# A two-block transformer kernel on one core: another order of feature tiles, steps moved between stages, and a rotation kept on one engine

## What is computed

```python
def first_block(x, c, ctx, c_ctx, ...):          # DEPTH = 2 layers
    for i in range(DEPTH):
        ml = modulation(c, w_mod[i], b_mod[i]);  mc = modulation(c_ctx, ...)
        hl = modulate(rmsnorm(xl, g_pre_mix[i]), ml[0], ml[1])
        hc = modulate(rmsnorm(xc, g_pre_mix[i]), mc[0], mc[1])
        # in-projection, conv branches, attention over context + latent keys, output product w_o
        xl_new = xl + ml[2] * rmsnorm(y_l, g_post_mix[i])
        h2 = modulate(rmsnorm(xl_new, g_pre_mlp[i]), ml[3], ml[4])
        xl_new = xl_new + ml[5] * rmsnorm(sqrelu_mlp(h2, w_mlp_in[i], w_mlp_out[i]), g_post_mlp[i])
        # the same for the context stream, except in the last layer
def second_block(x, ...):                        # 2 hybrid layers: delta rule, pooling, sparse attention
        q = apply_rope(rms_norm(qc, q_norm), cos_a, sin_a)
        k = apply_rope(rms_norm(kc, k_norm), cos_a, sin_a)
        return x + merged @ w_out
```

## Time and profile before

| what | value |
|---|---|
| three executions | 2986.65, 2987.75, 2988.89 us |
| median | 2987.75 us |
| profiled execution, its own time | 2985.46 us |
| its span in the trace | 2984.2 us |
| mean granted clock of TensorE | 0.984 of full |
| TensorE (PE) busy | 2854.2 us, 96% |
| DVE, ACT, POOL busy | 1361.4, 1125.9, 1309.4 us |
| read from memory | 286.93 MB, 97 GB/s over the span |

### The profile page before, as it was taken

One profiled execution on the slowest core, in us unless ns is written; L12 is line 12 of the kernel. 1 busy time (PEld: TensorE's weight loads), 2 busy tenths in 40 slices (PEclk: granted clock), 3 DMA queues, 4 the chain that ended last, 5 costly groups with the idle time before them and its releaser, 6 DMA issues.

```text
span 2984.2 us, 40937 instructions
## 1 busy us (share of the span) xinstructions
PE 2854.2 (96%) x16292; PEld 2354.3 (79%) x16292; DVE 1361.4 (46%) x2490; ACT 1125.9 (38%) x1909; POOL 1309.4 (44%) x860
## 2 busy tenths in 40 slices
PE   7789999999999999989999899999999999999999
PEld 6576777988888785778888787888878778888777
DVE  5447654232111475633111356775543368666432
ACT  4343554553322443543322344332333344323332
POOL 4253236774444441244444343344634443437433
PEclk9999999999999999999999999999999999999999
DMA  6833214553233323122333222111222221212222
GB/s 236 303 132 121 86 43 131 176 158 107 92 99 99 121 67 124 58 71 86 98 99 95 67 97 75 57 57 50 85 76 84 85 85 53 70 52 71 78 72 91
DMA packets 81982, 291.68 MB, mean 98 GB/s; under 512 B 9216, under 2 KB 9600, under 8 KB 81408
## 3 DMA queue, kind: packets, MB, share of 16 engines
q1 hardware_dynamic: 81792, 289.06, 29.3%
HBM read 286.93 MB, written 2.10 MB: 97 GB/s over the span
## 4 chain that ended last, share of the span: by engine, by line
PE 81%; DVE 11%; issue 3%; POOL 2%; ACT 2%; DMA 0%; SPq 0%; POOLq 0%; DVEq 0%; ACTq 0%
PE ps L595 61%; PE ps L568 6%; DVE ps L2186 4%; PE ps L738 3%; PE ps L623 2%; PE ps L759 2%; PE ps L990 1%; POOL t L2814 1%; PE ps L927 1%; PE ps L1001 1%; PE ps L863 1%; DVE t L2010 1%; POOL t L2834 1%; PE ps L1168 1%; DVE t L2476 1%
## 5 line engine op out<-in xcount | busy, mean ns | idle before, releaser
L595 PE MATMUL ps<-t,t 128*128 128x512 f32 (+3 forms) x9936 | 2215.4, 381 | 30.5 <-DVE t L1969 12.6
L595 PEld LDWEIGHTS ps<-t,t 128*128 128x128 f32 x9936 | 1783.3, 189 | 377.6 <-issue 42.9
L2814 POOL TENSOR_TENSOR t<-t,t 128x1024 fp32r<-128x1024 f32 (+3 forms) x444 | 1046.0, 2360 | 1101.6 <-ACT t L1303 1048.3
L1303 ACT ACTIVATE t<-t 128x1024 fp32r<-128x1024 f32 (+3 forms) x444 | 457.6, 1034 | 877.4 <-PE ps L595 826.1
L568 PE MATMUL ps<-t,t 128*128 128x128 f32 (+2 forms) x1676 | 245.8, 284 | 53.6 <-DVE t L2010 20.6
L568 PEld LDWEIGHTS ps<-t,t 128*128 128x128 f32 (+2 forms) x1676 | 196.9, 144 | 103.7 <-DVE t L2010 21.6
L2289 DVE TENSOR_TENSOR ps<-ps,t 128x512 f32<-128x512 f32 (+1 forms) x96 | 57.2, 605 | 335.3 <-ACT t L1591 331.5
L2302 DVE TENSOR_TENSOR t<-ps,t 128x512 f32<-128x512 f32 x60 | 40.9, 691 | 217.6 <-PE ps L595 217.5
L2834 POOL TENSOR_TENSOR t<-t,t 128x4 f32<-128x4 f32 (+2 forms) x93 | 85.7, 922 | 77.1 <-DVE t L1973 39.1
L2186 DVE SCALAR_TENSOR_TENSOR ps<-t,t,ps 128x512 f32<-128x512 f32 (+1 forms) x174 | 116.1, 667 | 6.7 <-ACT ps L1506 0.9
L738 PE MATMUL ps<-t,t 96*128 96x384 f32 (+1 forms) x320 | 108.9, 464 | 3.9 <-DVE t L2054 1.5
(11 more groups left out here) (258 smaller groups left out, 2471.6 us busy)
## 6 DMA issues: line engine op xcount, KB each, us to landing
t<-in_wbig SPq DMA_DIRECT2D x412, 512.0 KB, 3.5
t<-in_wmod SPq DMA_DIRECT2D x96, 512.0 KB, 6.6
t<-in_wbig SPq DMA_DIRECT2D x16, 416.0 KB, 3.2
t<-in_wbig SPq DMA_DIRECT2D x14, 256.0 KB, 2.7
t<-in_wbig SPq DMA_DIRECT2D x8, 332.0 KB, 2.8
t<-in_wbig SPq DMA_DIRECT2D x6, 384.0 KB, 3.0
t<-in_x SPq DMA_DIRECT2D x1, 2048.0 KB, 8.1
out<-t SPq DMA_DIRECT2D x8, 256.0 KB, 2.1
```

What stands on the lines that cost most here:

```text
L595: m = p.matmul(out, lhs, rhs, start=kk == 0 and n == 0, stop=kk == tiles - 1 and n == 2)
L1303: a.activation(c.hi(w), c.raw(w), ACT.Copy).then_inc(w_hi.h, w_hi.up(("cut", w)))
L2814: g.tensor_tensor(c.lo(w), c.raw(w), c.hi(w).bitcast(F32), ALU.subtract).then_inc(w_lo.h, w_lo.up(("cut", w)))
```

## The change

Eight parts, made in the programs of all engines alike:

1. `prep(l0)` and `prep(mc0)` go through the tiles in the order 4 to 7, 0 to 3; `high` of each waits only for the unit of `wo` that read that tile last; the first product of the stage starts with tile 4. Three more steps of the prep are placed inside `project`. Beside `project(c0)` the side steps go at rate 0.65 instead of 0.5.
2. `residual` multiplies by the row once before it takes the mean and three times after, and waits for the root only right before each addition.
3. In the last group of an MLP, the first step of the next prep on ACT, DVE and POOL (squares, mean, root) is placed ahead of the second in-product; TensorE's step stays.
4. Modulation group (0,4) moves from `heads(c0)` to the end of `mix(c0)`; (1,5) from `heads(l0)` to behind `zt` of c1; (1,10) and (1,11) from `heads(l1)` to behind `project(l1)`. Three of them get other ring slots and waits.
5. The row product for ml1 moves from ahead of `prep(ml1)` into `mlp(ml1)`.
6. During `zt` of c1 the units are cut 2, 2, 1 and 0 ahead instead of 2, 2, 2 and 2.
7. All four multiplications of the kc and qc rotations are DVE's.

```diff
+def first_tile(stage):
+    return 4 if stage[0] == "wo" or stage in (("cf", "l0"), ("w1", "mc0", 0, 0)) else 0
+def prep_order(n):
+    return (4, 5, 6, 7, 0, 1, 2, 3) if n in ("l0", "mc0") else tuple(range(8))
+def only(steps, n):
+    for _ in range(n):
+        next(steps)
+        yield
...
     def mod_slots(self, i, g):
-        return [4 * (n if n < 4 else 4 if n > 12 and n % 2 else 2 if n in (5, 7, 9) else 0) + q for q in range(4)]
+        return [4 * (n if n < 4 else {17: 3, 23: 1}.get(n, 4) if n > 12 and n % 2 else 2 if n in (5, 7, 9) else 0) + q
+                for q in range(4)]
...
 # ACT, POOL: product_gemm
-            cut(u, (1, 1, 2, 2)[kh] if stage == ("cf", "c0") else AHEAD)
+            cut(u, {("cf", "c0"): (1, 1, 2, 2), ("zt", "c1"): (2, 2, 1, 0)}.get(stage, (AHEAD,) * 4)[kh])
...
 # ACT: prep
             A.wait_ge(dve, ("pn", n, k))
+            if read and prep_order(n)[0]:
+                A.wait_ge(gemm, ("w", c.of[read][prep_order(n).index(k) // 2]))
...
-        if read:
+        ks = prep_order(n)
+        if read and not ks[0]:
             A.wait_ge(gemm, ("end", read))
-        high(0)
+        high(ks[0])
...
 # ACT, DVE, POOL: mlp
             for h in range(2):
+                if g == 3 and h:
+                    next(ahead, None)
                 yield from product_gemm(("w1", n, g, h), ...)
-            yield from weave(down(g), ahead, rate) if g == 3 else down(g)
+            yield from weave(down(g), chain((0,), ahead), rate) if g == 3 else down(g)
...
 # DVE: residual
         if row is not None:
-            for t in range(nt - 1):
-                gained(n, 1, t)
+            gained(n, 1, 0)
         V.wait_ge(act, ("ysq", n, 1, nt - 1))
...
         if row is not None:
-            gained(n, 1, nt - 1)
+            for t in range(1, nt):
+                gained(n, 1, t)
             V.wait_ge(dve, ("yg", n, 1, nt - 1))
-        V.wait_ge(pool, ("rr", n))
         for t in range(nt):
             for _ in range(apart):
                 yield
+            V.wait_ge(pool, ("rr", n))
...
 # DVE: rotate
+        if crossed is None:
+            v.tensor_tensor(tmp[2], p2, co, ALU.mult).then_inc(dve.h, dve.up())
+            v.tensor_tensor(tmp[3], p1, si, ALU.mult).then_inc(dve.h, dve.up())
...
-        V.wait_ge(pool, crossed)
+        if crossed is not None:
+            V.wait_ge(pool, crossed)
...
 # every engine's main program (PE's shown)
-    steps = beside(mix("c0"), g, (1, 2, 3, 9, 11, 13, 15))
+    steps = beside(beside(mix("c0"), g, (1, 2, 3, 9, 11, 13, 15)), mods(0, 4, 5, [2, 6]), (48,))
...
-    rest = onward(weave(heads("c0"), mods(0, 4, 12, [6, 7]), 0.45, -1.0), 2 * NH + 2)
+    rest = onward(weave(heads("c0"), mods(0, 5, 12, [6, 7]), 0.45, -1.0), 2 * NH + 2)
...
-    run(weave(project("c0"), both(rest, g, 4), 0.5))
-    next(g)
+    run(beside(weave(project("c0"), both(rest, g, 4), 0.65), only(g, 3), (11, 14, 15)))
     run(beside(weave(mix("l0"), g, 0.5), mods(1, 0, 1, [2, 6]), (56,)))
-    rest = onward(beside(heads("l0"), mods(1, 1, 6, [6, 7]), (4, 5, 12, 13, 20)), 4 * NH + 2)
+    rest = onward(beside(heads("l0"), mods(1, 1, 5, [6, 7]), (4, 5, 12, 13)), 4 * NH + 2)
...
-    run(weave(project("l0"), both(rest, g, 4), 0.45))
-    next(g)
+    run(beside(weave(project("l0"), both(rest, g, 4), 0.45), only(g, 3), (21, 24, 26)))
...
     keys = onward(mix("c1"), 8)
+    run(mods(1, 5, 6, main[2:4]))
     g = onward(prep("l1"), 5)
...
-    rest = onward(beside(heads("l1"), mods(1, 6, 12, [6, 7]), (4, 5, 12, 13, 20, 21)), 4 * NH + 2)
+    rest = onward(beside(heads("l1"), mods(1, 6, 10, [6, 7]), (4, 5, 12, 13)), 4 * NH + 2)
...
     run(weave(project("l1"), rest, 0.4))
-    row_of("ml1", 1, 1, 0)
+    run(mods(1, 10, 12, main[2:4]))
     g = onward(prep("ml1"), 5)
...
 # SP: fetch_mod
-        if i == 1 and g % 2:
+        if i == 1 and g in (1, 3, 7, 9):
             S.wait_ge(gemm, ("end", ("sb", "l1" if g > 6 else "l0")))
+        if i == 1 and g == 5:
+            S.wait_ge(dve, ("x", "l0", 3))
+        if i == 1 and g == 11:
+            S.wait_ge(turned, ("put", "l1", 0, 3))
```

More of the change, by code:

```diff
@@ L42, in mix @@
         for key in (("zt",) if n == "c1" else ("cf", "zt", "sc", "sb")):
-            block((key, n), "w_in", (i,), 0, 8, IN1[key])
+            for row in (512, 0) if (key, n) == ("cf", "l0") else (0, 512):
+                block((key, n), "w_in", (i,), row, 4, IN1[key])
         if n != "c1":
@@ L569, in turns, with product_gemm @@
         last.then_inc(turned.h, turned.up(*events))
-    def product_gemm(stage, mode, parts, T, w, tiles, ready, freed, first=0, banks=(0, 1, 2, 3)):
+    def product_gemm(stage, mode, parts, T, w, tiles, ready, freed, banks=(0, 1, 2, 3)):
         aH, aL = parts
@@ L1889, in act_program @@
     g = prep("l0")
-    run(weave(project("c0"), both(rest, g, 4), 0.5))
-    next(g)
+    run(beside(weave(project("c0"), both(rest, g, 4), 0.65), only(g, 3), (11, 14, 15)))
     run(beside(weave(mix("l0"), g, 0.5), mods(1, 0, 1), (56,)))
-    rest = onward(beside(heads("l0"), mods(1, 1, 6), (4, 5, 12, 13, 20)), 4 * NH + 2)
+    rest = onward(beside(heads("l0"), mods(1, 1, 5), (4, 5, 12, 13)), 4 * NH + 2)
     row_of("l0")
@@ L3001, in mlp @@
             for h in range(2):
+                if gr == 3 and h:
+                    next(ahead, None)
                 yield from product_gemm(("w1", n, gr, h), 4, 8, lambda b: None)
-            yield from weave(down(gr), ahead, rate) if gr == 3 else down(gr)
+            yield from weave(down(gr), chain((0,), ahead), rate) if gr == 3 else down(gr)
     def bc(col):
@@ L3156, in pool_program @@
     onward(steps, 2)
-    first = beside(mix("c0"), steps, (1, 2, 3, 9, 11, 13, 15))
+    first = beside(beside(mix("c0"), steps, (1, 2, 3, 9, 11, 13, 15)), mods(0, 4, 5), (48,))
     for n in (2, 3):
```

98 lines of the change are left out of this document (46 added, 52 removed).

## The result

The changed kernel takes 2968.26 us in the median of 4 runs (2965.27 to 2975.67), the kernel before 2988.32 beside it (4 runs, 2986.65 to 2990.79). The ratio is 0.9932, 95% interval 0.9921 to 0.9944: 20 us less. The profiled execution took 2965.27 us with a span of 2963.9, against 2985.46 and 2984.2 before.

What follows compares the result with a forecast made beforehand. TensorE, busy 2854.2 of 2984.2 us, was taken as the bound: its work plus some 130 us of waits. The terms summed to -27.5, from 2985.5 to 2958, on the median's scale 2960; range 2951 to 2973.

Steps and rivals of the forecast that it cites:

- root wait and squares ahead (D): In mc0: later root wait gains 2.3 us of TensorE's 2.66 wait; squares before ACT's cut cost net 2.4.
- heads(l0) without (1,5) (C): In heads(l0): the modulation group taken out gives back 1.93 us and 0.3 of transpose.
- heads(l1), ml1 (G+H): Two groups leave heads(l1), 4.4 us; the row product costs 1.95 in the MLP; net 2.5 gained, bounds 0 and 4.4.
- MLP update (E): In the MLP updates: three row products move behind the mean, taking about 0.5 us off the 9.3 wait.
- Rotations: Both layers: wait before the queries' transposes and slow pieces behind it go, 12 us; keys give 2 more.
- re-locked: Rival: cuts fall between DVE's six rotation instructions, the queries' wait stays, the 12 us are lost: 2972; chance 0.15.
- Start (part 4, group (0,4); part 1, rate): At project(c0): earlier bias transpose and full rate gain 3 of 3.5 us; moved group in mix(c0) gains 1, bounds 4 either way.
- With the wait two steps later DVE evicts first: In mc0's first group: DVE no longer stands for the root before evicting; 2.3 us of TensorE's 2.66 wait gained.
- Tile order: Starts of mix(l0) and mlp(mc0): waits of 2.52 and 2.26 us and slow units go, 4.1 and 3.5 gained, 7.6 together.
- Squares ahead: In mc0's last group: ACT's squares delay a cut, TensorE waits 4.5 us; root wait of 2.22 goes; net 2.4 lost.
- cuts in hand: Rival: mc0's squares and mix(l1)'s late cut are hidden, up to 9 us better, some 2953; chance 0.12.
- c1 and mix(l1): Additions faster, but squares stand behind the moved group's copy; mix(l1) starts 3.2 us later; net 1 us lost.

Runs made afterwards that it cites:

- no_order: Changed kernel with part 1 undone (tile order of loads, preparation and products, three early steps, rate): 2976.46 us, ratio 0.9955.
- no_rot: Changed kernel with part 7 undone, the crossed products of the kc and qc rotations back on GpSimd: 2984.02 us, ratio 0.9980.
- rest_only: Kernel before with parts 2 to 6 alone (changed kernel with parts 1 and 7 undone): 2989.64 us, ratio 0.9995.
- update_later: Changed kernel with the four update additions of l0 four steps apart instead of two: 2972.84 us, ratio 0.9947.
- after: The changed kernel itself, all seven parts, first measurement: 2968.26 us, ratio 0.9932 to the kernel before.
- after_again: The changed kernel run once more without any edit: 2973.12 us, ratio 0.9940.
- mod04_back: Changed kernel with modulation group (0,4) back inside heads(c0), the rest of part 4 as changed: 2969.74 us, ratio 0.9932.
- best: Changed kernel with mix(l1)'s first unit cut early, l0's update additions four steps apart, and part 3 undone: 2966.50 us, ratio 0.9926.
- no_squares_ahead: Changed kernel with part 3 undone, squares again behind the second in-product of the last MLP group: 2970.89 us, ratio 0.9934.

## Why the prediction was right, and where its terms were not

The forecast of 2960 (2951 to 2973) had the direction and the main mechanism. The likeliest case was 2955 to 2966; 2968.26 lies 2 above it. That the time fell inside the range is partly luck: the terms add up to 18.4 us by the table where 27.5 were forecast, so it is the width of the range that took it in, and the second measurement of the same kernel, 2973.12, stands at its upper edge. By the table its terms came out so, each the mean of the rows with the part less that of the rows without (F and G+H without the four rows whose start of mix(l1) was edited, D as given at no_order):

| term | predicted | measured |
|---|---|---|
| rotations (I, J) | -14 | -13.5 |
| tile order, mix(l0) (B) | -4.1 | -4.8 |
| tile order, mc0 (D) | -3.5 | -1.5 |
| root wait and squares ahead (D) | +0.1 | +1.0 |
| project(c0), group (0,4) (A) | -4 | +1.9 |
| heads(l0) without (1,5) (C) | -2.2 | -2.7 |
| start of mix(l1) (F) | +3.2 | +4.0 |
| heads(l1), ml1 (G+H) | -2.5 | -2.1 |
| MLP update (E) | -0.5 | -0.7 |
| sum | -27.5 | -18.4 |

- **Rotations: right in size, and better in the sum than in its two terms.** From the 16 transposes of the earlier trace rows to the end of the column, the rows with part 7 are 5.9 and 6.1 us shorter than the trace of before, just as worked out from it, but 4.7 and 4.5 shorter than no_rot and rest_only, whose slow stretches there are shorter: over the three 10.1, where the prediction had 12. What lies ahead of it in I and J, the keys among it, gave 3.4, where it had 2. No wait for L2057 is left before the queries' transposes. The rival "re-locked" was half seen: the lock still holds L2056 for 2.51 us and L2057 of the block before for 2.62. It doesn't decide, since each cut stops only one instruction of the six, as the prediction argued.
- **The failed step is "Start (part 4, group (0,4); part 1, rate)".** "With one group less in heads(c0) it comes earlier": it did, the bias transpose waits 0.41 instead of 2.22 at 157.73. But the wait of 2.24 before the third unit, which I let keep only some of it, stayed whole, where I had 3 of 3.5 gained. And the group at its new place costs a wait of 4.08 for its weights where one of 2.80 stood, a slow stretch and 1.56 behind it, while heads(c0) still waits 2.76 for weights. So the move cost 3.4 us of waits at the two places, nearer to the bound of 4 lost than to the 1 gained, and column A is 1.9 longer and not 4 shorter.
- **"With the wait two steps later DVE evicts first" holds only without part 1.** In no_order and rest_only the wait of 2.66 is 0.39, the 2.3 that I took. In the changed kernel it is 3.11. The three early steps of part 1 shorten the chain ahead of the update, so its first addition is due earlier, and again ahead of the evictions. I had costed parts 1 and 2 apart. update_later shows that mending it alone gives nothing, as the additions then hold a later eviction.
- **Tile order.** The waits went in both places. In mc0 the three preparation steps moved into project(l0) lengthen it (52.4 us from row product to first unit, 52.0 with the 2.26 of waiting in no_order). The wait for the cut is back (3.11 against 0.39), and the slow stretch has only moved, from the first wait of the earlier trace rows to the second, where the granted clock is now 0.57 from 484 to 488; the clock withheld 3.4 us over D in both.
- **Squares ahead: right in its mechanism**, 4.68 against the 4.5 worked out; the row's wait of 2.22 is gone. Two slips in the sums: the net of these terms is 2.3 and not 2.4, and the rival "cuts in hand" stands by its own terms, 9.3, at 2951 and not at 2953.
- **c1 and mix(l1):** the start was late as said, for the reason said; that part 6 could have been left out at no cost was not seen, though the prediction had written that the squares stand behind the group's copy.

## What to carry to other kernels

Cost the parts of a change together where they meet on one engine's order: a step that brings one instruction forward also brings forward whatever is queued behind it, and a wait that was moved behind the evictions came back ahead of them. Before making an operation faster, find what starts the next one; additions sped up by a third were worth nothing here, since the squares waited for something else, and the price was paid at the next unit. And where one execution differs from the next by as much as a part is worth, cut the traces at rows that all versions share, and compare means of stretches over every run that has the same code there.

## What the runs showed of the hardware

The same program on the same data meets different slow stretches from one execution to the next: after and after_again differ by 1.6 us in B (clock withheld 0.0 and 1.7) and by 3.2 in I (1.4 and 6.5), and by 0.1 or less in C, E and J. The same code in different kernels does so too. heads(l0), with the same waits to the hundredth at its start, took 122.7 us in four traces and 125.0 to 126.6 in eight; after and after_again are both among the four, so whether what runs ahead of it decides is not shown. TensorE of after, then of mod04_back, at that place:

```profile
293.43 0.42 PE L588 MATMUL ps<-t,t 128*96 128x128 f32 x2 [0.78 <-DVE t L2083]
294.37 1.56 PE L759 MATMUL ps<-t,t 96*128 96x384 f32 x4 [0.51 <-DVE t L2083]
```

```profile
291.34 0.66 PE L588 MATMUL ps<-t,t 128*96 128x128 f32 x2 [0.78 <-DVE t L2083]
292.52 2.92 PE L759 MATMUL ps<-t,t 96*128 96x384 f32 x4 [0.51 <-DVE t L2083]
```

The waits are alike, 0.78 and 0.51, and the products take 1.56 in one and 2.92 in the other, the granted clock being 1.00 in the first and 0.50 from 292 to 296 in the second. So a wait near 2.2 us in front of the same products can cost the wait alone (best) or another 1.7 us withheld by the clock (no_squares_ahead), and shortening one of two waits gave nothing while shortening both gave 3.6. Over the five executions of after_again the mean clock goes from 0.985 to 0.981 as the time goes from 2968.29 to 2977.12.
